# A second norm in two halves: gains multiplied in ahead of the root, row stores ahead of the third weight set, the last gate behind the expert loads

## The reference, cut to what matters

```python
x = x + g1 * mix
hffn = rms_norm(x, p['norm_ffn'][l]) * (1 + sc2) + sh2      # per token: 1/sqrt(mean(x*x) + EPS)
x = x + g2 * hier_moe(hffn, l, p)

# hier_moe: top-1 of 4 groups, top-2 of the 4 experts in it, 16 experts in all
hid = silu(einsum('td,edf->tef', x, moe_w_gate)) * einsum('td,edf->tef', x, moe_w_up)
out = einsum('tef,efd->td', hid * gates[:, :, None], moe_w_down)
```

## Time and profile before

| | |
|---|---|
| median of 3 runs | 732.18 us (732.04 to 733.64) |
| profiled execution, its time | 731.23 us |
| its span (first to last instruction) | 729.4 us |
| mean granted TensorE clock, share of full | 0.924 |
| PE, DVE, ACT, POOL busy share of the span | 83%, 73%, 46%, 19% |
| DVE work of `modulated`, lines 1662 and 1663 | 5 x 1.28 us and 5 x 1.22 us |
| size of one weight load, one row store, one gather | 1024 KB, 512 KB, 512 KB |
| size of the `g2t` broadcast | 2 x 512 KB |

### The profile page before, as it was taken

How to read it: one execution, slowest core, us unless ns; L and a number is a source line. 1 busy time by engine, 2 the same in 40 slices (tenths; PEclk the granted TensorE clock), 3 DMA queues, 4 the chain that set the end, 5 groups by cost and what they waited for, 6 DMA issues and landing times.

```text
span 729.4 us, 8211 instructions
## 1 busy us (share of the span) xinstructions
PE 608.6 (83%) x3202; PEld 484.6 (66%) x3202; DVE 531.1 (73%) x663; ACT 337.6 (46%) x446; POOL 135.4 (19%) x86
## 2 busy tenths in 40 slices
PE   0879999999989969999799999912999999999420
PEld 0359878999868646555678888702888887888320
DVE  1592698999997676888862600786899888888467
ACT  4142124321104635556655211560488777886442
POOL 0002000007992000000223422002122211102140
PEclk9889999999999959999999999955899999999765
DMA  7964749965002100000344300297589999996773
GB/s 273 411 246 156 265 173 332 364 207 173 1 9 75 58 1 0 1 0 1 117 173 155 116 1 1 112 388 281 195 354 419 421 417 420 419 420 249 248 271 144
DMA packets 45486, 147.05 MB, mean 202 GB/s; under 512 B 7296, under 2 KB 16100, under 8 KB 37768
## 3 DMA queue, kind: packets, MB, share of 16 engines
q1 hardware_dynamic: 35112, 116.25, 41.7%
q0 software_dynamic: 5472, 20.45, 7.4%
q10 hardware_dynamic: 4864, 9.84, 3.5%
HBM read 126.44 MB, written 20.09 MB: 201 GB/s over the span
## 4 chain that ended last, share of the span: by engine, by line
PE 48%; DVE 26%; DMA 14%; ACT 6%; issue 4%; ACTq 1%; POOL 0%; SPq 0%; DVEq 0%; POOLq 0%
PE ps L552 8%; DMA m_raw<-in_moe_w_gate_dram 8%; PE ps L554 8%; PE ps L553 7%; DVE cy L1414 5%; DMA raw<-in_w_ada_dram 4%; PE ps L698 3%; PE ps L827 2%; PE ps L830 2%; PE ps L829 2%; DVE gu_lo L1801 2%; DMA h_rows<-h2k 2%; DVE w_lo L1372 2%; PE ps L534 2%; ACT gu_hi L1147 2%
## 5 line engine op out<-in xcount | busy, mean ns | idle before, releaser
L1414 DVE SCALAR_TENSOR_TENSOR cy<-cu,tapw,cy 128x655 f32<-128x655 f32 x120 | 113.9, 949 | 3.4
L1801 DVE TENSOR_TENSOR gu_lo<-m_raw,gu_hi 128x2048 fp32r<-128x2048 f32 x36 | 82.2, 2290 | 19.9 <-ACT gu_hi L1147 19.6
L1147 ACT ACTIVATE gu_hi<-m_raw 128x2048 fp32r<-128x2048 f32 x36 | 68.8, 1917 | 18.1 <-DMA m_raw<-in_moe_w_gate_dram 16.9
L827 PE MATMUL ps<-gu_hi,xt_h 128*128 128x512 f32 x144 | 60.2, 418 | 8.5 <-DVE gu_lo L1801 8.4
L552 PE MATMUL ps<-w_hi,mix 128*128 128x512 f32 x160 | 62.8, 392 | 2.8 <-DVE w_lo L1613 2.8
L829 PEld LDWEIGHTS ps<-gu_lo,xt_h 128*128 128x128 f32 x288 | 56.1, 195 | 12.7
L1303 POOL TENSOR_TENSOR w_lo<-raw,w_hi 128x2048 fp32r<-128x2048 f32 x7 | 32.7, 4676 | 170.3 <-ACT w_hi L1076 170.3
L574 PE MATMUL ps<-hT,w_hi 128*128 128x320 f32 x192 | 60.1, 321 | 3.9 <-DVE hT L1395 3.9
L554 PE MATMUL ps<-w_hi,mix 128*128 128x512 f32 x160 | 62.3, 389 | 0.0
L553 PE MATMUL ps<-w_lo,mix 128*128 128x512 f32 x160 | 62.3, 389 | 0.0
L575 PE MATMUL ps<-hT,w_hi 128*128 128x320 f32 x192 | 59.0, 315 | 0.0
(11 more groups left out here) (337 smaller groups left out, 1388.9 us busy)
## 6 DMA issues: line engine op xcount, KB each, us to landing
raw<-in_w_ada_dram SPq DMA_DIRECT2D x24, 1024.0 KB, 7.9
m_raw<-in_moe_w_gate_dram SPq DMA_DIRECT2D x18, 1024.0 KB, 10.4
m_raw<-in_moe_w_up_dram SPq DMA_DIRECT2D x18, 1024.0 KB, 13.2
m_raw<-in_moe_w_down_dram SPq DMA_DIRECT2D x18, 1024.0 KB, 14.8
raw<-in_w_in_dram SPq DMA_DIRECT2D x11, 1024.0 KB, 8.7
y_rows<-ys ACTq DMA_DIRECT2D x17, 512.0 KB, 8.9
raw<-in_w_out_dram SPq DMA_DIRECT2D x8, 1024.0 KB, 5.3
y_rows<-pool_u POOLq DMA_DIRECT2D x1, 5120.0 KB, 26.6
```

Source lines behind the costliest of these rows:

```text
L827: pe.matmul(out, xt_h[q][:, k, :], gu_hi[q][:, k, :], start=(k == 0), stop=False)
L1147: act.activation(gu_hi[q][:, :, u * FF:(u + 1) * FF], m_raw[3 * s + u][:, :].rearrange("p (k n) -> p k n", k=KB), ACT.Copy).then_inc((g_hi ...
L1414: ins = dve.scalar_tensor_tensor(out=cy[:, blk, :], in0=cu[:, blk, i:i + CY], scalar=w, in1=cy[:, blk, :], op0=MUL, op1=ADD)
L1801: dve.tensor_tensor(gu_lo[s][u][:, :, :], m_raw[3 * s + u][:, :].rearrange("p (k n) -> p k n", k=KB), gu_hi[q][:, :, u * FF:(u + 1) * FF]. ...
```

## The change

Five edits:

1. The multiplication by `gain2t` leaves `modulated` and becomes `gained(t)`, one instruction per tile, which does not need the root. Tiles 0 to 2 are done right behind their `mixed(1, t)`, tile 3 behind `mixed(1, 4)`, tile 4 behind the second `variance`. `modulated(t)` is then one instruction: `h2k * rs_x + sh2t`.
2. On SP all five row stores stand ahead of set 2.
3. The `g2t` broadcast moves behind the expert loads, ahead of the loop over further tiles.
4. On ACT, `square(1, 4)` goes ahead of `rows_out_T(4)`, and `root(3, TT, 3)` ahead of the two copies of the logits.
5. `h2k` moves to the start of `HL`, so that it can be written while the last projection weights are still in use; `gu_hi` swaps its two regions, and the waits follow: ACT waits for the stores of rows 0 to 3 ahead of expert 1's weights, where it waited for row 0 ahead of expert 0's down weights.

```diff
-    h2k = [at(f"h2k{t}", [D], o) for t, o in enumerate((RAW + 8192, HL + 16384, HL + 20480, HL + 24576, HL + 28672))]
+    h2k = [at(f"h2k{t}", [D], o) for t, o in enumerate((HL, HL + 4096, HL + 8192, HL + 12288, HL + 16384))]
-    gu_hi = [at(f"gu_hi{q}", [KB, 2 * FF], R, f32r) for q, R in enumerate((HL, RAW))]
+    gu_hi = [at(f"gu_hi{q}", [KB, 2 * FF], R, f32r) for q, R in enumerate((RAW, HL))]
...
+        def store_rows(t):
+            sp.wait_ge(h2_made, t + 1)
+            sp.dma_start(h2_rows[t * P:(t + 1) * P, :], h2k[t][:, :]).then_inc(tile_moved[t], 16)
+
         for i in range(SETS):
             for m in range(3):
                 load_weights(sp, i, i, m)
-            for t in range(2 * i, min(2 * i + 2, TT)):
-                sp.wait_ge(h2_made, t + 1)
-                sp.dma_start(h2_rows[t * P:(t + 1) * P, :], h2k[t][:, :]).then_inc(tile_moved[t], 16)
-        sp.wait_ge(sq_made, 3 * TT)
-        for cnd in range(2):
-            sp.dma_start(g2t[:, cnd, :], row[cnd, 3].partition_broadcast(P)).then_inc(g1_in, 16)
+            for t in ((0, 1), (2, 3, 4), ())[i]:
+                store_rows(t)
...
                 load_weights(sp, i - 1 + SETS if i - 1 + SETS < NE else first_e, raw_set(i - 1), 2)
+        for cnd in range(2):
+            sp.dma_start(g2t[:, cnd, :], row[cnd, 3].partition_broadcast(P)).then_inc(g1_in, 16)
         with sp.Fori(0, extra) as r:
...
         square(1, 3)
-        for t in range(2, TT):
-            rows_out_T(t)
+        rows_out_T(2)
+        rows_out_T(3)
         square(1, 4)
+        rows_out_T(4)
+        root(3, TT, 3)
         logits_out(1, 0, LT)
         logits_out(2, LT, TT)
-        root(3, TT, 3)
...
-        act.wait_ge(tile_moved[0], 32)
         down_hi(0)
+        for t in range(LT):
+            act.wait_ge(tile_moved[t], 32)
         gate_up_hi(1, 0)
...
         def modulated(t):
             cnd = 0 if t < LT else 1
-            link(dve.scalar_tensor_tensor(out=h2k[t][:, :], in0=x[:, t, :], scalar=rs_x[:, t:t + 1], in1=gain2t[:, cnd, :], op0=MUL, op1=MUL))
-            dve.tensor_tensor(h2k[t][:, :], h2k[t][:, :], sh2t[:, cnd, :], ADD).then_inc(h2_made, 1)
+            dve.wait_ge(h2_gain, t + 1)
+            dve.scalar_tensor_tensor(out=h2k[t][:, :], in0=h2k[t][:, :], scalar=rs_x[:, t:t + 1], in1=sh2t[:, cnd, :], op0=MUL, op1=ADD).then_inc(h2_made, 1)
+
+        def gained(t):
+            dve.wait_ge(wo_used, 6)
+            dve.tensor_tensor(h2k[t][:, :], x[:, t, :], gain2t[:, 0 if t < LT else 1, :], MUL).then_inc(h2_gain, 1)
...
+        dve.wait_ge(tiles_in, 5 * 16)
         for t in range(3):
             mixed(1, t)
+            dve.wait_ge(x2_made, TT + t + 1)
+            gained(t)
         variance(0, 3)
         mixed(1, 3)
         dve.wait_ge(rs_raw, 2)
         refine(rs_x[:, 0:3], var_x[:, 0:3], nw[:, 0:3])
-        dve.wait_ge(tiles_in, 5 * 16)
         modulated(0)
         mixed(1, 4)
+        dve.wait_ge(x2_made, TT + 4)
+        gained(3)
         modulated(1)
         variance(3, TT)
+        dve.wait_ge(x2_made, TT + 5)
+        gained(4)
         modulated(2)
```

More of the change, by code:

```diff
@@ L264, in build @@
         "wo_hi wo_lo wo_used mo_ps x2_made")
-    h2_made, x2T_ps, x2T_made, lg_ps, wrc_step = sems("h2_made x2T_ps x2T_made lg_ps wrc_step")
+    h2_gain, h2_made, x2T_ps, x2T_made, lg_ps, wrc_step = sems("h2_gain h2_made x2T_ps x2T_made lg_ps wrc_step")
     gsub_made, gexp_made, A_made, rank_ps, slots_made, hot_made, idx_ps, idx_made, np_made, iota_in = sems(
```

## The result

| | before | changed |
|---|---|---|
| median of the runs beside each other | 732.91 us (732.04 to 734.99, 4 runs) | 725.41 us (724.14 to 726.60, 4 runs) |
| profiled execution | 731.23 us | 725.82 us |
| its span | 729.4 us | 723.9 us |
| mean granted clock | 0.924 | 0.933 |

The ratio is 0.9887, 95% interval [0.9866, 0.9909]: 1.1% faster. The forecast was 728.0 us, a gain of 4.2; the runs gained 7.5.

A forecast was written before the change was run, and what follows sets the result against it. Bound: DMA saturated at 419 GB/s from 560 us, its start set by the first expert, waiting on row 4's store and `idx`. First gather 6.6 us earlier, less 2.4 contention: 732.18 - 4.2 = 728.0 us; range 725.4 to 730.8.

The forecast's parts named there:

- I take 504.0 for the first and 505 for the second.: Landing times in us of the first two gathers beside set 2; contention takes 2.4 of the 6.6 us gained.
- the 9.8 us of the saturated stretch: Median gather time under full DMA load, 11.3 us at most; taken as upper bound for the first gathers.
- the byte sum: Rows 2 to 4, set 2 and two gathers, 5.77 MB from 490.65 on, take 13.8 us: all landed by about 504.5.
- The lower bound: First gathers as fast as before, 5.4 us from issue to landing: first one landed at 501.5.
- Rival B: Queues take turns, first gathers land nearly as if alone, some 1.3 us more each: gain 5.5 to 6.6, 726.2 us; chance 0.17.
- I let this [the clock] move with the work.: PE's clock rises 8.5 us behind the first transposes as before; a rise 3.5 us off would gain or lose 1.7 us.
- At its old place it delayed nothing that anybody waited for: gain 0.: The `g2t` broadcast's old place behind row 4 on SP's queue held up nobody, so leaving it gains 0.
- DVE: DVE saves 1.4 us to the logits and 2.4 behind them, 3.8 in sum, so `idx` is ready at 495.85.
- The cover for ACT: Expert 1's weight copies wait for rows 0 to 3, start at 493.1, end at 499; 7 us before ACT's next instruction.
- `g2t` in the tail: Broadcast behind the last expert loads adds 2.5 us of all engines ahead of the last gather; cost 0, at most 0.4.
- Every later step earlier by the same: From `gate_up(0)` at 508.4 on, every later step comes 4.2 us earlier, through the saturated stretch to the end.
- The median: Median of the runs falls by the same 4.2 us, from 732.18 to 728.0 us.

The follow-up runs named there:

- b_hold: Kernel before, with DVE's first `gate_up_lo(0, 0)` held until POOL has issued its first two gathers; one run, 732.57 us beside 731.94 of before.
- b_split: Changed kernel with SP's order of before, so only the norm's factors and ACT's order changed; median 730.98 us, ratio 0.9960 to before.
- a_late2_hold: Changed kernel with set 2's loads issued only after both first gathers landed, and DVE's first `gate_up_lo` held until POOL issued both; single run, 726.73 us.
- a_g2t_old2: Changed kernel with the `g2t` broadcasts put back behind set 2 on SP's queue, timed; ratio 0.9938 [0.9917, 0.9960] to before.
- a_g2t_old: Changed kernel with the `g2t` broadcasts put back behind set 2 on SP's queue; single run, 736.39 us.
- a_g2t_old_hot: Changed kernel with the `g2t` broadcasts back behind set 2, plus unread products in PE's idle stretches to hold its clock; single run, 725.71 us.
- the hot pair: Changed kernel and kernel before, each with unread products in PE's gaps to hold its clock; 725.23 us (median, ratio 0.9885) and 731.95 us (one run).
- b_stores_g2t: Kernel before with row 4's store ahead of set 2 and the `g2t` broadcasts behind the expert loads; median 728.63 us, ratio 0.9936.

## Why the prediction was wrong, point by point

The place and the kind of the gain were right: the first gather starts 6.7 us sooner (forecast 6.6), the store of row 4 leaves the chain and `idx` stands in its place, contention takes part of it back, and the expert part behind it follows. The size was wrong in two terms, the time from the gather's start to its landing (7.85 us, measured 6.51) and the clock (0 in the sum, measured 1.85 to the first silu), both in the direction of too little.

- **"I take 504.0 for the first and 505 for the second."** This is the step that failed at the landing: 7.85 us from the gather's start at 496.15, where it took 6.51. The value was not worked out but chosen between two bounds, with more weight on the 9.8 us of the saturated stretch and close to the end of the byte sum. The lower bound, "the first two gathers ran with the DMA engines to themselves, and took 5.4 us", had the engines right, but DVE held the issue: alone it is 4.4 (`b_hold`, `b_split`, `a_late2_hold`). Contention adds 2.1 to that, not the 3.5 that 7.85 would need. The byte sum, too, ended late: it had everything landed by 504.5, and the gathers' last packet moves at +49.1, which is 503.7 on that scale. `gate_up(0)` came 5.6 us earlier, not 4.2.
- **Rival B** had the right size at that point, 5.5 to 6.6 us, partly by luck: its 5.4 and 1.3 us make 6.7 against 6.51 measured, from a base that was 1.0 us too long and a contention that was too small (1.3 against 2.1, and 3.6 with the 1 MB more, 7.97 - 4.4). Its shares were right. Equal turns are the rule of the Trainium skill ("DMA: Bandwidth & Descriptors", Queues, rings and completion order), and the packets agree: in the first 3 us in which the gathers move, they get 0.59 MB beside 0.64 of loads in `a_g2t_old2`, 0.64 beside 0.61 in `a_g2t_old`, and 0.52 beside 0.73 in `a_g2t_old_hot`. What B lacks is the wait ahead of the first packet, 1.4 us in the changed kernel and 2.5 with the 1 MB more. The saturated stretch, on which the forecast leaned against it, was the wrong comparison.
- **"I let this [the clock] move with the work."** It rose 4.0 us behind the first transposes instead of 8.5. The prediction had its price, up to 1.7 us, in the range and not in the sum. It stood at nothing in the sum, on no other ground than that it would move with the work; by the row of the milestones it is 1.85 us, the largest part of the 2.84 us that were missed, and by the hot pair 1.15 us at the end. What decides when it rises is not settled: one kernel ran twice and took 8.24 and 6.66 us to the silu.
- **"At its old place it delayed nothing that anybody waited for: gain 0."** True of the kernel before, false of the changed one. A gain of 0 was read from the profile in which the gather started late. In the changed kernel the broadcast would lie under the gather: 1.5 us at the landing, in two profiles. In the median it is 0.2 to 0.5% (0.9938 [0.9917, 0.9960] against 0.9887 [0.9866, 0.9909] and, run again, 0.9916 [0.9880, 0.9951]); the first pair of intervals lies just apart, the second overlaps. The sum had the right bytes in it, since it left `g2t` out of the 5.77 MB, so this did not move the forecast; the attribution was wrong.
- **DVE** gained 4.4 us instead of 3.8: 1.93 to the logits, where I had 1.4, and 2.51 behind them, where I had 2.44. The 0.5 are mostly ACT's new order, to which I gave 0.4; without it `idx` is 0.7 later. POOL then needed 0.87 us from `idx` (0.80 "issue" in the chain), not 0.3. The two errors cancel, which is luck: the gather's start was right to 0.1 us.
- **The cover for ACT** held. Expert 1's first copy starts at 494.61 behind row 3's store, +38.50, where the forecast had +38.53, and its last ends 6 us ahead of the next instruction:

```profile
494.61 3.71 ACT L1150 ACTIVATE gu_hi<-m_raw 128x2048 fp32r<-128x2048 f32 x2 [10.98 <-DMA h_rows<-h2k]
498.23 1.89 ACT L1156 ACTIVATE d_hi<-m_raw 128x2048 fp32r<-128x2048 f32 x1
506.12 1.02 ACT L1175 ACTIVATE xt_h<-ps 128x1024 fp32r<-128x1024 f32 x1 [6.00 <-PE ps L819]
```

- **`g2t` in the tail** cost nothing that could be seen: no wait of PE for the last gather, as at the earlier trace rows.

```profile
651.55 0.95 SPq L489 DMA_DIRECT2D g2t<-mod_rows  x2
```

```profile
656.21 0.97 POOL L1329 DMA_INDIRECT xg<-h_rows,idxc  x1
```

```profile
669.61 1.05 PE L819 MATMUL ps<-ident,xg 128*128 128x128 f32 x8
```

- **"Every later step earlier by the same":** nearly. 0.43 us of the lead is lost between the first silu and the end. `b_stores_g2t` loses none (208.86) and `a_g2t_old2` does (209.57), so it is not the broadcast in the tail; more is not known.
- **The median** moved 7.5 us where the profiles from the anchor give 7.04. 30 executions of before lay between 727.4 and 736.6 us, so the half us is within the noise.

## What to carry to other kernels

A duration "alone" is only that if no other engine held the instruction: look at what the neighbour engine ran while it was issued, and at the shortest of its kind, before it becomes the base of a sum. A transfer that nobody waits for is free only as long as nothing urgent starts while it is queued; if the change makes something start earlier, price again all that lies in the queue at the new time. And where two conditions meet at one instruction, edits must be priced together: here the gather started 2.2 and 0.1 us sooner apart, and 6.7 together. A term that "moves with the work", as the clock, needs a reason before it goes into a sum at nothing. And how two queues share the engines can be read from the packets of each in the stretch, ahead of any estimate from landings.

## What was not expected of the hardware

- An indirect gather whose issue starts on POOL inside a DVE `TENSOR_TENSOR` of 128x2048 with both inputs in SBUF (2.28 us) ends 0.8 to 1.0 us behind it, whenever it started: the first two issues took 1.64 to 2.91 us so, against 0.95 to 1.08 free. DVE is not held by the gather's issue (4.52 against 4.49 us for two).
- Beside a full queue of 1 MB loads a 512 KB gather took 6.5 to 8.0 us instead of 4.4. Once its packets move, it gets about half of the bytes (0.59 of 1.23 MB in 3 us); the larger part of the delay, 1.4 to 2.5 us, lies ahead of its first packet, and why is open.
- POOL starts the first gather 0.87 us behind the end of DVE's `idx`. A later one starts 0.28 us behind the end of PE's transposes (510.45, with their end at 510.17, in before). What makes the difference is open.
- 102 and 124 products without use in PE's gaps (`a_hot2` and `b_hot2`) kept the granted clock at 1.00 instead of 0.50 ahead of the first expert, and shortened the time from its first product to the silu by 1.9 us in before, and by nothing in the changed kernel, where the clock was up in time. Its gain there came before: the transposes to `gate_up(0)` took 3.62 us instead of 4.43.
